# Feed-forward products over x high and x low side by side: three streams of 346 columns in place of four of 260

## What is computed

```
xn = rms_norm(x, g_mix);  z = xn @ w_in          # then attention heads and a gated recurrence
x = x + mix @ w_out
hf = rms_norm(x, g_ffn) @ w_up                   # 2048 x 8192
x = x + square(relu(hf)) @ w_down                # 8192 x 2048
y = rms_norm(x, g_final)
```

## Time and profile before

| | |
|---|---|
| Time, median of 3 runs | 2487.22 us (2480.38 to 2491.83) |
| Profiled execution, its own time | 2486.51 us |
| Span of the profile | 2484.6 us |
| PE busy | 2390.2 us, 96% |
| PEld busy | 2321.3 us, 93% |
| DVE busy | 1130.0 us, 45% |
| ACT busy | 705.0 us, 28% |
| Granted clock of PE, mean | 0.982 |

### The profile page before, as it was taken

One profiled execution on the slowest core, in us unless ns is written; L12 is line 12 of the kernel. 1 busy time (PEld: TensorE's weight loads), 2 busy tenths in 40 slices (PEclk: granted clock), 3 DMA queues, 4 the chain that ended last, 5 costly groups with the idle time before them and its releaser, 6 DMA issues.

```text
span 2484.6 us, 49629 instructions
## 1 busy us (share of the span) xinstructions
PE 2390.2 (96%) x20689; PEld 2321.3 (93%) x20689; DVE 1130.0 (45%) x1163; ACT 705.0 (28%) x829; POOL 325.7 (13%) x267
## 2 busy tenths in 40 slices
PE   6998999999998999999999999999999999999996
PEld 5997888888887999999999999999999999999996
DVE  5347776677774488333333232332332333333332
ACT  5223432333334423221221221221211212212233
POOL 0023344333442223000000000000000000000011
PEclk9999999999999999999999999999999999999998
DMA  6356988778884533322322323323323233233321
GB/s 217 101 158 204 324 280 281 259 270 305 278 283 136 186 116 111 87 101 85 95 92 84 101 84 87 99 87 94 89 97 88 84 101 84 84 101 85 91 87 77
DMA packets 355614, 352.52 MB, mean 142 GB/s; under 512 B 11764, under 2 KB 319381, under 8 KB 354373
## 3 DMA queue, kind: packets, MB, share of 16 engines
q1 hardware_dynamic: 328484, 279.65, 35.7%
q0 software_dynamic: 18608, 67.64, 7.9%
q10 hardware_dynamic: 8448, 4.20, 0.6%
HBM read 338.49 MB, written 12.94 MB: 141 GB/s over the span
## 4 chain that ended last, share of the span: by engine, by line
PE 78%; DVE 7%; issue 5%; POOL 3%; DVEq 2%; ACT 1%; DMA 1%; POOLq 1%; SPq 0%; ACTq 0%
PE PS L1466 49%; PE PS L1470 24%; POOL KR L514 3%; DVE SC L1121 2%; DVE KR L1119 2%; DMA KR<-in_cache_k 1%; PE PS L1608 1%; DVE WL L981 1%; DVEq L1255 1%; POOLq L496 1%; PE PS L1704 1%; DVE NM L1254 0%; ACT WH L575 0%; PE PS L1649 0%; POOL KR L497 0%
## 5 line engine op out<-in xcount | busy, mean ns | idle before, releaser
L1466 PE MATMUL PS<-XH,WH 128*128 128x260 f32 x3872 | 800.5, 288 | 21.9 <-DVE WL L981 9.8
L1466 PE MATMUL PS<-XL,WH 128*128 128x260 f32 x3872 | 785.2, 285 | 0.0
L1470 PE MATMUL PS<-XH,WL 128*128 128x260 f32 x3872 | 784.4, 284 | 0.0
L1466 PEld LDWEIGHTS PS<-XH,WH 128*128 128x128 f32 x3872 | 602.6, 191 | 39.9 <-issue 24.0
L1470 PEld LDWEIGHTS PS<-XH,WL 128*128 128x128 f32 x3872 | 602.9, 190 | 0.0
L1466 PEld LDWEIGHTS PS<-XL,WH 128*128 128x128 f32 x3872 | 602.8, 190 | 0.0
L981 DVE TENSOR_TENSOR WL<-RAW,WH 128x2048 fp32r<-128x2048 f32 x185 | 424.9, 2297 | 260.4 <-ACT WH L575 260.3
L575 ACT ACTIVATE WH<-RAW 128x2048 fp32r<-128x2048 f32 x185 | 354.3, 1915 | 621.4 <-PE PS L1470 621.3
L1466 PE MATMUL PS<-HH,WH 128*128 128x260 f32 x2048 | 413.2, 283 | 0.0
L1470 PE MATMUL PS<-HH,WL 128*128 128x260 f32 x2048 | 412.6, 283 | 0.0
L1466 PE MATMUL PS<-HL,WH 128*128 128x260 f32 x2048 | 412.0, 283 | 0.0
(11 more groups left out here) (275 smaller groups left out, 1155.9 us busy)
## 6 DMA issues: line engine op xcount, KB each, us to landing
KR<-in_cache_k POOLq DMA_DIRECT2D x128, 512.0 KB, 5.0
VR<-in_cache_v SPq DMA_DIRECT2D x128, 512.0 KB, 6.0
RAW<-in_w_up SPq DMA_DIRECT2D x128, 512.0 KB, 5.0
RAW<-in_w_down SPq DMA_DIRECT2D x128, 512.0 KB, 4.0
RAW<-in_w_in SPq DMA_DIRECT2D x82, 512.0 KB, 5.3
RAW<-in_w_out SPq DMA_DIRECT2D x32, 512.0 KB, 5.0
xT_spill<-A SPq DMA_DIRECT2D x1, 4160.0 KB, 13.3
VR<-xT_spill SPq DMA_DIRECT2D x16, 260.0 KB, 3.8
```

Source lines behind the costliest of these rows:

```text
L1466: mm(dsts[c], wh(k), x[:, k, c * HT:(c + 1) * HT], start=first and n == 0 and x is xh, stop=False)
L1470: ins = mm(dsts[c], wl(k), xh[:, k, c * HT:(c + 1) * HT], start=False, stop=last and n == len(kts) - 1)
```

## The change

XH and XL now lie in one tile XX, a row of 2T = 1040 columns for each k, and HH and HL in one tile HX. For the feed-forward part a row is ordered as the first half of high (260), low columns 0 to 85, the second half of high (260), then the other low columns: 86 to 259 and 260 to 519. Three streams of 346, 346 and 348 columns run over this row under one WH block, into three banks. The first two banks thus hold a half of the high sum in columns 0 to 259 and low sums behind it. WL adds to the first two banks in 260 columns, as before. A k-step is five matmuls with 1560 columns, where it was six with 1560.

Tiles now alternate between two trios of banks (0 to 2, 3 to 5). The low sums must be added to the high ones: ACT copies them to the new tile TL (`low_sums`), DVE adds PSUM and TL to RT and then does the max and the product as a second operation; for down tiles it adds TL to A and then PSUM to A (`add_wide`). `ffn_lo` and the writing of the low part of HX each become three operations. All up tiles (64) and the down tiles of seven chunks (112) are changed. The down tiles of the last chunk keep `products` with six matmuls, now over HX in flat order, and their first one waits until the last trio is emptied too.

```
+    LA = (2 * T // 3) // 2 * 2 - HT
+    WD = HT + LA
+    WIDTHS = (WD, WD, 2 * T - 2 * WD)
+    WIDE_LO = ((0, LA, HT, 0), (LA, HT, HT + WD, LA), (HT, T, WD + 2 * HT - LA, WD))
...
+            def low_sums(c, n, s):
+
+                trio, w = at(T_F + s, c * (TC // 2) + n)
+                act.wait_ge(tile_done, 2 * w + trio + 1)
+                act.wait_ge(tile_out[trio], w)
+                nc.scalar.activation(halves(TL[:, s, 0:2 * LA]), PS[:, 3 * trio:3 * trio + 2, HT:WD], ACT.Copy)
+                nc.scalar.activation(TL[:, s, 2 * LA:T], PS[:, 3 * trio + 2, 0:T - 2 * LA], ACT.Copy).then_inc(tl_ready, 1)
...
             def ffn_lo(a):
                 k = OUT_ORDER[a]
                 dve.wait_ge(xh_ready, 2 * KD + a + 1)
-                V.scalar_tensor_tensor(XL[:, k, :], A[:, k, :], PRM[:, R_GFFN + k:R_GFFN + k + 1], XH[:, k, :].bitcast(F32),
-                                       ALU.mult, ALU.subtract).then_inc(xl_ready, 1)
+                for t0, t1, dst, hi in WIDE_LO:
+                    ins = V.scalar_tensor_tensor(XX[:, k, dst:dst + t1 - t0], A[:, k, t0:t1], PRM[:, R_GFFN + k:R_GFFN + k + 1],
+                                                 XX[:, k, hi:hi + t1 - t0].bitcast(F32), ALU.mult, ALU.subtract)
+                ins.then_inc(xl_ready, 1)
...
                     slot = tile_wait(T_F + s, c * (TC // 2) + j)
-                    V.scalar_tensor_tensor(RT[:, s, :].rearrange("p (a t) -> p a t", a=2), pair_view(slot), 0.0,
-                                           RS[:, :].rearrange("p (a t) -> p a t", a=2), ALU.max, ALU.mult)\
-                        .then_inc(tile_out[slot], 1)
+                    dve.wait_ge(tl_ready, TC * c + 2 * j + s + 1)
+                    V.tensor_tensor(halves(RT[:, s, :]), wide_view(slot), halves(TL[:, s, :]), ALU.add).then_inc(tile_out[slot], 1)
+                    dve.drain()
+                    V.scalar_tensor_tensor(RT[:, s, :], RT[:, s, :], 0.0, RS[:, :], ALU.max, ALU.mult).then_inc(rt_ready, 1)
...
+            def add_wide(k, c, n, m):
+
+                slot, w = at(T_F + m, c * (TC // 2) + n)
+                dve.wait_ge(tl_ready, TC * c + 2 * n + m + 1)
+                a = row(A, k)
+                V.tensor_tensor(a, a, TL[:, m, :], ALU.add)
+                dve.drain()
+                V.tensor_tensor(halves(a), wide_view(slot), halves(a), ALU.add).then_inc(tile_out[slot], 1)
...
+            def wide_products(x, wh, wl, bank, kts, insert={}, ready=None):
+
+                for n, k in enumerate(kts):
+                    if ready and n in ready:
+                        pe.wait_ge(*ready[n])
+                    for c, width in enumerate(WIDTHS):
+                        mm(PS[:, bank + c, 0:width], wh(k), x[:, k, c * WD:c * WD + width], start=n == 0,
+                           stop=c == 2 and n == len(kts) - 1)
+                    for f in insert.get(n, ()):
+                        f()
+                    for c in range(2):
+                        ins = mm(PS[:, bank + c, 0:HT], wl(k), x[:, k, c * WD:c * WD + HT], start=False, stop=n == len(kts) - 1)
+                return ins
...
+                            if isinstance(j, int) and s == 0 and m == 0:
+                                pe.wait_ge(tile_out[1 - pair], at(T_F + CH + 1, c * (TC // 2))[1])
```

More of the change, by code:

```diff
@@ L198, in hymba_step @@
         RK = sb("RK", [P, TT + 1], scope=ffn_scope)
-        HH = sb("HH", [P, CH, T], F32R, ffn_scope)
-        HL = sb("HL", [P, CH, T], F32R, ffn_scope)
+        HX = sb("HX", [P, CH, 2 * T], F32R, ffn_scope)
+        TL = sb("TL", [P, 2, T], scope=ffn_scope)
         ffn_scope.close()
@@ L276, in one, with row, hi_halves, wide_view @@
             return bass.ds(i, 1)
+        def row(t, k):
+            return t[:, k, :] if isinstance(k, int) else t[:, one(k), :].rearrange("p a t -> p (a t)")
+        def hi_halves(t, k, wide):
+            r = row(t, k)
+            if wide:
+                return r[:, 0:2 * WD].rearrange("p (c n) -> p c n", c=2)[:, :, 0:HT]
+            return r[:, 0:T].rearrange("p (c n) -> p c n", c=2)
+        def wide_view(trio):
+            return PS[:, 3 * trio:3 * trio + 2, 0:HT]
+        def halves(ap):
+            return ap.rearrange("p (c n) -> p c n", c=2)
         def pair_view(pair):
@@ L904, in _, with up @@
                 ffn_hi(OUT_ORDER[a])
-            def up(c, j, first=False):
+            def up(c, j, first=False, wide=True):
                 for s in range(2):
@@ L910, in up @@
                     if first and s == 0:
-                        root(3, RS[:, :], 4, KD)
-                    slot, w = at(T_F + s, c * (TC // 2) + j)
-                    act.wait_ge(tile_out[slot], w + 1)
+                        root(3, RS[:, :], 6, KD)
+                    low_sums(c, j, s)
+                    act.wait_ge(rt_ready, CH * c + 2 * j + s + 1)
                     act.wait_ge(hl_ready, CH * c + 2 * j + s + 1)
@@ L916, in up @@
                     act.drain()
-                    nc.scalar.activation(HH[:, one(2 * j + s), :].rearrange("p a t -> p (a t)"), HF[:, s, :], ACT.Copy)\
+                    nc.scalar.activation(hi_halves(HX, 2 * j + s, wide), halves(HF[:, s, :]), ACT.Copy)\
                         .then_inc(h_ready, 1)
@@ L927, in chunk @@
                         split_hi(U_F + CH + 1 + s, c * (UC // 2) + j, TC * c + 4 * j + (T_F + CH + 2 * s))
+                        for m in range(2):
+                            low_sums(c, 2 * j + (CH // 2 + s), m)
             chunk(0, True)
@@ L932, in _ @@
             with act.Fori(0, CH // 2) as j:
-                up(NC - 1, j)
+                up(NC - 1, j, wide=False)
             def y_rows(k):
@@ L1814, in residual_sums @@
                 for c in range(2):
-                    ins = mm(PS[:, 4 + c, 0:HT], ones[:, :], ACC[:, c * HT:(c + 1) * HT], start=True, stop=True)
+                    ins = mm(PS[:, 6 + c, 0:HT], ones[:, :], ACC[:, c * HT:(c + 1) * HT], start=True, stop=True)
                 ins.then_inc(ss_done, 1)
@@ L1819, in up @@
                 for s in range(2):
-                    if first and s == 0:
-                        unit(U_F, 0, T_F, 0, {21: [residual_sums]}, kts=OUT_ORDER,
-                             ready={a: (xl_ready, 2 * KD + a + 1) for a in range(KD)})
-                    else:
-                        unit(U_F + s, c * (UC // 2) + j, T_F + s, c * (TC // 2) + j)
+                    head = first and s == 0
+                    slot, w = at(U_F + s, c * (UC // 2) + j)
+                    trio, tw = at(T_F + s, c * (TC // 2) + j)
+                    pe.wait_ge(lo_done, 2 * w + slot + 1)
+                    pe.wait_ge(tile_out[trio], tw)
+                    wide_products(XX, lambda k: WH[slot][:, k * P:(k + 1) * P], lambda k: WL[slot][:, k * P:(k + 1) * P], 3 * trio,
+                                  OUT_ORDER if head else range(KD), {10: [residual_sums]} if head else {},
+                                  {a: (xl_ready, 2 * KD + a + 1) for a in range(KD)} if head else None).then_inc(tile_done, 1)
             def down(c, j, rows=None):
```

32 lines of the change are left out of this document (19 added, 13 removed).

## The result

| | before | after |
|---|---|---|
| Median | 2486.05 us (17 runs, 2480.38 to 2491.83) | 2492.32 us (17 runs, 2488.28 to 2502.14) |
| Ratio to before, with its 95% interval | | 1.0025 [1.0015, 1.0034] |
| Profiled execution, its own time | 2486.51 us | 2488.28 us |
| Span | 2484.6 us | 2486.4 us |
| DVE busy, ACT busy | 45%, 28% | 51%, 33% |

A forecast was written before the change was run, and what follows sets the result against it. Feed-forward time taken as PE-bound, number of matmuls by their spacing. 2486.5 - 22.3 + 3.1 + 1.5 + 0.8 + 1.4 + 1.75 = 2472.8 us for the profiled execution, so 2473 as median; range 2445 to 2496.

The forecast's parts named there:

- I take them as fixed: Feed-forward matmuls: 9.2 of the 11.8 ns beside the columns don't grow with width, so dropping one matmul a k-step gains 22.3 us.
- the first rival: Feed-forward matmuls: the cost goes with the columns, only 2.6 ns fixed; gain 4.9 us, stalls stay, 2490 us; chance 0.21.
- slower: Feed-forward wide streams: 346 columns cost more than their columns, for instance from starting at byte 1384; 2507 at 3 ns; chance 0.10.
- long stream hides more: Feed-forward wide streams: 346 columns, longer than their load, have only 2.6 ns beside them; gain 74.2 us, 2422 us; chance 0.17.
- The waits: PE stalls added into the feed-forward part, in the w_out product, at first down tiles and last chunk, clock included: 8.55 us.
- The way into the feed-forward part: Ahead of the third up tile: longer low-part blocks and RT in two operations delay PE by 3.1 us (2.2 to 4.2).
- The idle ahead of the third tile: PE ahead of the third up tile: idle 3.7 us, from 3.1 added, 0.2 of before and 0.4 from arriving earlier.
- The w_out product: In the w_out product, DVE at its limit: longer `ffn_lo` operations add 0.8 us (0 to 2).
- The last chunk: Last chunk's first down tile waits until the last trio is emptied: 1.75 us, once.
- The first down tiles of seven chunks: Last k-step of each chunk's first down tile waits for the eighth low part: 0.2 us each, 1.4 in all (0 to 2.5).
- The clock: After PE's idle ahead of the third up tile, a lower granted clock costs up to 3 us; taken as 1.5.
- What is hidden: Up tiles and down units: ACT's and DVE's added work, about 8.1 and 4.9 us, fits within 11.3 us of PE work.

The follow-up runs named there:

- e1: Probe behind the changed kernel's last sums, stages of 192 matmuls of differing widths and formats: one-pass 260 columns 120.8 ns, 512 columns 231.7 ns, bf16 512 columns 215.8 ns.
- e2: Changed kernel with streams of 352, 352 and 336 columns in place of 346, 346 and 348: 2481.64 us, ratio to before 0.9974.
- e10: e6 with streams of 368, 368 and 304 columns in place of 352, 352 and 336: 2474.58 us, ratio to before 0.9953.
- e7: e6 with the change's own widths of 346, 346 and 348 columns: 2488.43 us, ratio to before 1.0011.
- e8: Probe at the changed kernel's end, mixed starts and k-steps of eight width choices: 721.8 ns for 346, 715.3 for 352, 713.3 for 368.
- e4: Probe behind the changed kernel, streams from various start bytes: 346 columns took 157.3 ns from byte 1384 and 158.3 from 2768.
- e11: Probe at the changed kernel's end, 346 columns from three starts over chosen rows of HX: 157.8 ns over rows 0 and 4, 160.0 over all.
- e6: e2 with the third up tile's weights made earlier and the last chunk's first down tile in banks 3 and 4: 2479.49 us, ratio to before 0.9971.

## Why the prediction was wrong, point by point

**The step that failed** is "I take them as fixed". It made 22.3 us of gain out of 11.8 ns a matmul, and a k-step 0.3 to 0.4 ns longer was measured. Two things stand in its place. First, of the 11.8 ns only 1 to 6 are fixed (e1), so that is about what a merge can give: e2 and e10 have k-steps 5.6 and 7.1 ns shorter than before, places in memory included. This is the first rival, whose 2490 was near the 2492 measured, with a fixed cost of 2.6 ns that lies inside the measured range. Second, widths of 346, 346 and 348 columns give even that back: against 352 they cost 6 ns a k-step, 10 us in all (e2, e7, e8). The rival "slower" had 1.6 ns a wide matmul, near the 1.5 by which three starts exceed one in e1, but its cause is wrong, since byte 1384 by itself costs nothing (e4), and the time stayed below its bound of 0.5%. That the first rival's sum lies within 2 us of the measured time is partly luck: the waits, clock included, were 3.4 us smaller than forecast, and the cost of the widths, which that rival does not have, made up for it.

**The reason I gave** was that plain float32 agrees with the clock to 1%, and that a column should not cost 4% more in the one-pass format alone. The first half is right (219.2 ns), the second wrong: at 512 columns the one-pass stream costs 8.6% more than the clock, and bf16 1.2%.

**Right:** that the load is not what sets 120 ns. With 128 columns, where the load sets the pace, the spacing is 111.4 ns, forecast 113, and a load of 8 columns in place of 128 takes off 2.5 ns at 260 columns. So the rival "long stream hides more" is out: a 346-column stream takes 158 to 160, not 146.8.

**The waits** and the clock behind them, 8.55 us forecast, were 5.2 in the trace. The way into the feed-forward part: forecast 3.1, measured 0.87 + 2.02 less the 0.2 of before, 2.7; its place was wrong in part, for a third of it stood ahead of the second tile. The idle ahead of the third tile, forecast at 3.7 us, was 2.02. The w_out product: 0.8, measured near 0.8 (waits of 0.28 and 0.38, and a slower first matmul behind each, x4 in 0.71 where others have 0.65). The last chunk: 1.75, measured 1.69. The first down tiles of seven chunks: 1.4, measured nothing; I had put the chain at 5.0 to 5.2 us, and it took 4.86 (1070.51 to 1075.37), so the low part stood ready 0.18 us ahead of the last k-step. The clock: 1.5, measured 0 in after and 1.5 in one execution of e2.

**What is hidden** was right: DVE is busy for 83 us in 200, ACT for 59 to 62, and no wait of PE stands between the third up tile and the last chunk.

**Open.** What makes the widths of 346 slow is not settled. The spacing goes with the places of the streams in memory, and places that agree in a block of 256 bytes give the same (e11, rows 0 and 4). The tested starts by themselves, theories A and B with their blocks of 128 and 64 bytes, and a cost of moving to another row fail, and no rule that fits all stages was found. Making the WL products in bf16, which e1 would put at 9 ns less a matmul, was not tried.

## What to carry to other kernels

Before merging streams to save "overhead per matmul", measure the spacing at two widths: one width can't tell a fixed cost from a slower column. Here the split was 1 to 6 ns fixed against 11.8 assumed, which took a forecast gain of 22 us down to one that a poor choice of widths could wipe out. Then try several widths of the merged stream: going from 346 to 352 or to 368 columns, a change of one constant, was worth 10 and 14 us (e7 against e6 and e10), more than all the waits that the change added.
